# The last level of a blockwise triangular inverse, done on one quarter of the matrix

## The reference, cut to what matters

```python
lmat = jnp.where(tril_strict, jnp.einsum('bnhid,bnhjd->bnhij', k_beta, k) * decay, 0.0)
t_inv = lax.linalg.triangular_solve(eye + lmat, jnp.broadcast_to(eye, lmat.shape),
                                    left_side=True, lower=True, unit_diagonal=True)
u = jnp.einsum('bnhij,bnhjd->bnhid', t_inv, v_beta)
w = jnp.einsum('bnhij,bnhjd->bnhid', t_inv, k_beta * jnp.exp(g)[..., None])
```

## Time and profile before

| what | value |
|---|---|
| median of 3 runs | 2967.79 us (2967.61 to 2977.02) |
| the profiled execution | 2968.09 us |
| span of its trace | 2966.3 us |
| the scan, about | from 554 us to 1270 us of the span |
| PE busy over the span | 2681.6 us (90%) |
| DVE, ACT, POOL busy | 1400.3, 1040.5, 606.5 us |

### The profile page before, as it was taken

How to read it: one execution, slowest core, us unless ns; L and a number is a source line. 1 busy time by engine, 2 the same in 40 slices (tenths; PEclk the granted TensorE clock), 3 DMA queues, 4 the chain that set the end, 5 groups by cost and what they waited for, 6 DMA issues and landing times. The chain is left out here.

```text
span 2966.3 us, 46114 instructions
## 1 busy us (share of the span) xinstructions
PE 2681.6 (90%) x18134; PEld 2525.5 (85%) x18134; DVE 1400.3 (47%) x2320; ACT 1040.5 (35%) x1801; POOL 606.5 (20%) x489
## 2 busy tenths in 40 slices
PE   7999999589898999828999869989999999999999
PEld 3898999578888888726777758889999999999999
DVE  3565331157666766447888833352222242222222
ACT  4312332233343333136778733322222222222211
POOL 1001222434333433143323221210111000111100
PEclk9999999779897999858999979999999999999999
DMA  5324664334343433140000044332222233222232
GB/s 202 144 80 131 220 220 153 101 91 111 100 151 80 122 85 86 59 163 14 9 17 16 12 181 166 116 99 71 78 78 71 78 114 94 71 78 72 69 96 70
DMA packets 194779, 294.22 MB, mean 99 GB/s; under 512 B 82704, under 2 KB 121648, under 8 KB 192816
## 3 DMA queue, kind: packets, MB, share of 16 engines
q1 hardware_dynamic: 191728, 276.15, 29.6%
q10 hardware_dynamic: 2880, 15.73, 1.5%
HBM read 228.28 MB, written 63.52 MB: 98 GB/s over the span
## 5 line engine op out<-in xcount | busy, mean ns | idle before, releaser
L277 PE MATMUL f_ps<-mf_h_hi,mf_w_hi 128*128 128x320 f32 x1408 | 435.1, 309 | 1.4 <-PEq L1982 1.4
L277 PE MATMUL f_ps<-mf_h_hi,mf_w_lo 128*128 128x320 f32 x1408 | 435.1, 309 | 0.0
L277 PE MATMUL f_ps<-mf_h_lo,mf_w_hi 128*128 128x320 f32 x1408 | 435.1, 309 | 0.0
L2415 DVE TENSOR_TENSOR mf_w_lo<-mf_w_raw,mf_w_hi 128x1024 fp32r<-128x1024 f32 (+1 forms) x135 | 188.8, 1399 | 431.6 <-ACT mf_w_hi L2267 431.4
L277 PE MATMUL proj_ps<-h_hi,w_hi 128*128 128x320 f32 x896 | 282.7, 316 | 6.0 <-DVE w_lo L575 5.6
L277 PE MATMUL proj_ps<-h_hi,w_lo 128*128 128x320 f32 x896 | 278.0, 310 | 0.0
L277 PE MATMUL proj_ps<-h_lo,w_hi 128*128 128x320 f32 x896 | 278.0, 310 | 0.0
L277 PEld LDWEIGHTS f_ps<-mf_h_hi,mf_w_hi 128*128 128x128 f32 x1408 | 264.4, 188 | 1.6 <-issue 1.6
L277 PEld LDWEIGHTS f_ps<-mf_h_lo,mf_w_hi 128*128 128x128 f32 x1408 | 264.4, 188 | 0.0
L277 PEld LDWEIGHTS f_ps<-mf_h_hi,mf_w_lo 128*128 128x128 f32 x1408 | 264.4, 188 | 0.0
L2341 POOL TENSOR_TENSOR f_ff_lo<-f_ff_f,f_ff_hi 128x640 f32 (+1 forms) x44 | 69.3, 1576 | 783.1 <-ACT f_ff_hi L2267 783.1
(11 more groups left out here) (323 smaller groups left out, 6425.2 us busy)
## 6 DMA issues: line engine op xcount, KB each, us to landing
mf_w_raw<-w_up_dram SPq DMA_DIRECT2D x88, 512.0 KB, 3.5
w_ada_raw<-w_ada_dram SPq DMA_DIRECT2D x16, 1024.0 KB, 5.2
mf_w_raw<-w_mix_dram SPq DMA_DIRECT2D x32, 512.0 KB, 5.0
w_raw<-w_in_dram SPq DMA_DIRECT2D x28, 512.0 KB, 5.1
mf_w_raw<-w_down_dram SPq DMA_DIRECT2D x32, 448.0 KB, 3.3
delta_t<-delta_tile ACTq DMA_DIRECT2D x10, 1024.0 KB, 6.7
fill_raw<-w_in_dram SPq DMA_DIRECT2D x20, 512.0 KB, 4.2
kq_t<-delta_t SPq DMA_DIRECT2D x20, 512.0 KB, 4.3
```

Source lines behind the costliest of these rows:

```text
L277: ins = nc.tensor.matmul(out, w(k), a(k), start=(first and n == 0 and q == 0), stop=(last and n == len(ks) - 1 and q == 2))
L2415: nc.vector.tensor_tensor(wlo[:, slot, 0:nk], raw[:, slot, 0:nk], whi[:, slot, 0:nk].bitcast(F32), ALU.subtract).then_inc(E[half]["lo"], 1)
```

## The change

At level 6 the two 64-row blocks on the diagonal are already inverted, and only the quarter that joins them is new: below the diagonal in one direction, above it in the other. The changed kernel computes that quarter alone. `quarters(u)` gives the two halves of the partitions as p and q.

- The product into `bank_A` takes 64 rows (p) of both operands and 64 moving columns.
- VectorE copies only the quarter, by a plain copy, 64 partitions by 256 elements. The mask of level 6 is gone, and `levels_sb` is a third smaller.
- The products into `banks_bc` take the 64 rows q of both operands, still 128 stationary columns, and 64 moving columns.
- ScalarE copies two quarters, one from each half of `banks_bc`, by two instructions of 64 partitions by 256 elements. The other quarters stay in `x_inv` as level 5 left them.

```diff
@@ vector @@
-                            nc.vector.tensor_tensor(Y[:, c], bank(a), idn(keep["levels"][:, lv - LV[0], u % 2]), ALU.mult).then_inc(e["a_out"], 1)
+                            if lv < LV[-1]:
+                                nc.vector.tensor_tensor(Y[:, c], bank(a), idn(keep["levels"][:, lv - LV[0], u % 2]), ALU.mult).then_inc(e["a_out"], 1)
+                            else:
+                                p, q = quarters(u)
+                                nc.vector.tensor_copy(Y[q, c, :, p], bank(a)[q, :, 0:HD]).then_inc(e["a_out"], 1)
@@ scalar @@
-                            nc.scalar.activation(XX[:, c].rearrange("p t h i -> p t (h i)"), BC[c][:], ACT.Copy).then_inc(e["x_ready"], 1)
+                            if lv < LV[-1]:
+                                nc.scalar.activation(XX[:, c].rearrange("p t h i -> p t (h i)"), BC[c][:], ACT.Copy).then_inc(e["x_ready"], 1)
+                            else:
+                                p, q = quarters(u)
+                                nc.scalar.activation(XX[q, c, 0, :, p], bankB(c)[q, :, 0:HD], ACT.Copy)
+                                nc.scalar.activation(XX[p, c, 1, :, q], bankC(c)[p, :, 0:HD], ACT.Copy).then_inc(e["x_ready"], 1)
@@ tensor @@
+                            p, q = quarters(u)
                             for m in range(H4):
-                                last = mm(bank(a)[:, m], NI[:, u % 2, c, m], src(0, c, m))
+                                if lv < LV[-1]:
+                                    last = mm(bank(a)[:, m], NI[:, u % 2, c, m], src(0, c, m))
+                                else:
+                                    last = mm(bank(a)[:, m, 0:HD], NI[p, u % 2, c, m], XX[p, c, 0, m, p])
...
                             for m in range(H4):
-                                mm(bankB(c)[:, m], src(1, c, m), Y[:, c, m])
-                                last = mm(bankC(c)[:, m], Y[:, c, m], src(1, c, m))
+                                if lv < LV[-1]:
+                                    mm(bankB(c)[:, m], src(1, c, m), Y[:, c, m])
+                                    last = mm(bankC(c)[:, m], Y[:, c, m], src(1, c, m))
+                                else:
+                                    mm(bankB(c)[:, m, 0:HD], XX[q, c, 1, m], Y[q, c, m, p])
+                                    last = mm(bankC(c)[:, m, 0:HD], Y[q, c, m], XX[q, c, 1, m, q])
```

More of the change, by code:

```diff
@@ L819, in delta_scan @@
         col = lambda u, at, n=8: tab[:, u % 2, tile(u), at:at + n]
+        quarters = lambda u: (slice(0, 64), slice(64, 128)) if u % 2 == 0 else (slice(64, 128), slice(0, 64))
         a_index, z_index = {}, {}
@@ L2572, in build @@
                 keep["offdiag"] = sb2("offdiag_sb", [P, P])
-                keep["levels"] = sb2("levels_sb", [P, LEVELS - 4, 2, P])
+                keep["levels"] = sb2("levels_sb", [P, LEVELS - 5, 2, P])
                 delta_scan(nc, io, keep, tab, h_hi[0], h_lo[0])
@@ L2589, in constants @@
     tri = np.stack([tri, tri.T], 1)
-    levels = np.zeros((P, LEVELS - 4, 2, P), np.float32)
-    for lv in range(4, LEVELS):
+    levels = np.zeros((P, LEVELS - 5, 2, P), np.float32)
+    for lv in range(4, LEVELS - 1):
         s = 2 ** lv
```

## The result

The changed kernel takes 2989.57 us (median of 14 runs, 2977.64 to 3018.27) against 2967.84 us for the kernel before, beside which it ran: a ratio of 1.0087, 95% interval 1.0069 to 1.0104. It is 22 us slower. The forecast of 2970.5 us was wrong, and the time lies above its range of 2959 to 2980 us.

A forecast was written before the change was run, and what follows sets the result against it. It took the diagonal blocks' loop through VectorE, SyncE and memory to bound 14 units, TensorE's program with VectorE's copies the others. All terms were 0 except +2.6 us for changes of form: 2968.09 + 2.6 = 2970.7, stated as 2970.5 us, range 2959 to 2980.

The forecast's parts named there:

- VectorE's and ScalarE's copies: Level 6 copies: 0.27 us saved each on VectorE, 0.27 to 0.33 on ScalarE, none on the path; value 0.
- The products themselves: Level 6's 24 products a unit: weight loads set the 0.111 us distance, so halving the columns gives 0.
- Rival B: Level 6: 64-row products on one half don't overlap; 3045 us, or 2978 if only the load comes bare; chance 0.08 together.
- The changes of form: TensorE at level 6, going between 128 and 64 rows: the engine empties; 0.44 us a unit with fill.
- What of it counts: Level 6's delay disappears where VectorE waits for its blocks, stays in seven units: +2.6 us, bounds 0 to +7.8.
- 17 x 0.44 + 0.3: Upper bound for the level 6 delay over the scan, if none is absorbed: +7.8 us.
- the loop's: Diagonal blocks' round through VectorE, SyncE and memory, claimed to set the period in 14 units of the scan.
- rival C: TensorE's clock in the scan: 6.2 us per half-clock stretch; one either way 0.2, two or more slower 0.10, faster 0.05.
- How the numbers follow: The prediction's list of chances: forecast 0.72, B 0.08, C's slower side 0.10, A's second case 0.04, C's faster 0.05.
- C's slower side: Two or more additional half-clock stretches on TensorE in the scan, two giving 2983 us; chance 0.10.

The follow-up runs named there:

- e1: Against the kernel before, only the level 6 copies are quarters; the products stay 128 rows by 128 columns: 2965.55 us, ratio 0.9993.
- e3: The changed kernel with 128 rows given back to the level 6 products, 64 moving columns kept: 2974.86 us, ratio 1.0026 against the kernel before.
- e4: The changed kernel with full 128x128 products into `bank_A`, those into `banks_bc` as changed: 2974.42 us, ratio 1.0025 against the kernel before.
- e5: The changed kernel with three useless 128-row, 512-column products in TensorE's wait ahead of level 6: 2970.55 us, ratio 1.0029 against the kernel before.
- e11: The changed kernel with the fill between the two groups into `banks_bc` moved ahead of both, 16 products in one piece: 3001.01 us, ratio 1.0113.
- e15: The changed kernel with 128 moving columns, 64 rows kept, and the fill moved ahead of both `banks_bc` groups: 2986.30 us, ratio 1.0082.
- e7: e1 with 64 rows for the last head of each group only, 6 of 24 products a unit: 2984.03 us, ratio 1.0069 against the kernel before.
- e13: e1 with the fill between the two groups into `banks_bc` moved ahead of both: 2965.77 us, ratio 1.0008 against the kernel before.

## Why the prediction was wrong

- **VectorE's and ScalarE's copies, 0 us.** Right: e1 is 0.9993, at equal clock 1 us from before. Durations of 0.43 and 0.38 us as forecast.
- **The products themselves, 0 us.** Right: 0.11 us apart in the rows above, and e3 at equal clock is at 2968.4. Rival B (64-row loads that don't overlap) is out.
- **The changes of form, 0.44 us a unit.** The sum is nearly right, 0.50 measured, its parts less so: 0.165 into `banks_bc` where 0.25 stood, 0.144 out where 0.07 stood. The rule that the prediction weighed (the Trainium skill, TensorEngine Tiling (Array Packing), section "Key Properties") holds here, at about 0.15 us a change.
- **What of it counts, +2.6 us (0 to 7.8).** Not settled. At 0.34 us for each us at half clock, the kernels with 64-row products are 3 to 9 us over before, and the change itself 7.6, nearly all of 17 x 0.44 + 0.3. At the 0.45 of the earlier trace rows it is 1 or 2 us, below the forecast. The wait for the blocks after, beside its row and over the same stretch, is now met in 10 units and not 14:

```profile
DVE diag_inverse L1165 <- DMA diag_blocks<-diag: 21.8, 10, 9.0
```

  So fewer units have a wait that could absorb a delay. A unit that has lost clock may be TensorE's and no longer the loop's; that is argued only, and no run separates it.
- **The clock, rival C.** This is the step that failed. I put the clock at nothing in the sum, took it as chance, about as likely to move one way as the other, and gave 0.10 to two or more stretches more. What the runs show is a push in one direction: 54 us more at half clock (387 against 333), 18 to 25 of 26 us. What should have told me stood in the rows: TensorE stands for over 1 us just ahead of the changed products (the 1.34 us there are the weight load's; the first product waits 1.08), the change puts short breaks and narrower products right behind this wait, and unit 14 showed what a fall costs. e4 and e5 bear the place out in part: full products behind the wait leave 17 of the 54 us, and filling the wait brings the changed kernel to 338 us. But the kernel before goes to 305 by the same filling, so 33 us of the push don't need the wait. Three more units with such a stretch, at the 6.2 us of that row, would have made 2970.7 + 18.6 = 2989 us.
- **The chances.** The list under "How the numbers follow" adds up to 0.98 and not to 1. Nothing hangs on it.

The Trainium skill, TensorE: Matmul & The Clock Gate, section "A second HAM failure mode: psum-queue depth-cycling", says that frequent short idling between groups of matmuls can be enough to make the clock swing. This case's trace agrees in part: waits of 1.05 to 1.73 us stand ahead of the falls at level 6 in units 2, 3, 7, 13 and 14 of after, and waits of 1.06 to 1.07 us in units 1, 6, 10, 11 and 12 have none. The prediction didn't weigh that section; by it C's slower side should have had more than a chance of 0.10.

What stays open: what at level 6 pushes the clock down where the wait is filled, and why 64-row products in one piece seem to cost more clock than in two (e11, e15), when they have fewer breaks. e7 says that it is not their number, and by e13 the order alone does little. No kernel here has 64-row products without a change of form beside them, so the emptying and the rows can't be told apart for good. Nor was it tried to shorten the wait itself rather than fill it.

## What to carry to other kernels

Where TensorE bounds a kernel and runs near its full clock, ask of each edit not only what it takes off TensorE but whether it leaves the engine emptier, above all next to a place where it already waits: here the breaks and the smaller products cost at most 0.4 us a unit directly and some 0.9 or more by the clock (7.6 and 18 us over 20 units). Fewer rows or columns in a product didn't make TensorE faster where its pace was that of the weight loads, 0.11 us a product. And look at the granted clock in every comparison: two kernels compared at equal half-clock time show what an edit costs, and the rest shows what it does to the clock; a wait filled with useless products of full size gave 0.35% on the kernel before. Set it beside the same filling in the other kernel, or it looks like a cure for the edit when it helps both.

## What was not expected of the hardware

- Halving the moving columns of the products, with the same distance of 0.11 us between products, put 31 us more of the run at half clock (e3, 364 against 333 us, or 339 on its own chip). The quarter copies that e3 has as well did nothing by themselves (e1).
- Six 64-row products a unit, with two changes of form more, cost as much as 24 (371 and 369 us).
- A us at half clock costs some 0.34 us between runs and not 0.5, probably since part of the time at 1.2 GHz lies where TensorE isn't the bound; in unit 14 of the earlier trace rows it cost 0.45.
- 64-row products into `banks_bc` and 64-row key products overlap: in unit 4 of after the first load for the key products stands between two of `banks_bc`. The rows are TensorE's loads:

```profile
762.20 0.19 PEld L1221 LDWEIGHTS banks_bc<-y_res,x_inv 64*128 64x128 f32 x1
...
762.24 0.18 PEld L1221 LDWEIGHTS bank_A<-kq_t 64*128 64x128 f32 x1
762.31 0.19 PEld L1221 LDWEIGHTS banks_bc<-x_inv,y_res 64*128 64x128 f32 x1
762.34 0.19 PEld L1221 LDWEIGHTS bank_A<-kq_t 64*128 64x128 f32 x1
762.43 0.19 PEld L1221 LDWEIGHTS banks_bc<-y_res,x_inv 64*128 64x128 f32 x1
```

Two streams of loads at 0.10 to 0.12 us each run beside one another there, and no break stands between the one and the other.
